# Block 0's last two output tiles as one pair by seven products, in a hybrid decoder kernel

## The reference

```python
u = rms_norm(h, g_mix[i])
z = u @ w_in[i]
...
h = h + jnp.concatenate([y_lru, y_pool], axis=-1) @ w_out[i]
v = rms_norm(h, g_ffn[i])
up = causal_dwconv(v @ w_up[i], w_conv_ffn[i], b_conv_ffn[i])
h = h + (jax.nn.gelu(gate) * val) @ w_down[i]
...
h = h + jax.nn.sigmoid(q @ w_ple_gate[i] + b_ple_gate[i]) * (p[i] @ w_ple_proj[i])
```

## Time and profile before

| | before |
|---|---|
| runs | 2138.32, 2137.21, 2137.34 us |
| median | 2137.34 us |
| the profiled execution's own time | 2137.18 us |
| its span, first to last instruction | 2135.4 us |
| granted TensorE clock, mean | 0.997 |
| TensorE busy | 2111.9 us (99%), 9274 matmuls |
| VectorE busy | 1511.0 us (71%) |
| ScalarE busy | 880.2 us (41%) |
| GpSimd busy | 380.9 us (18%) |
| HBM | 250.75 MB read, 175.11 MB written |

### The profile page before, as it was taken

The page is one execution under the profiler, slowest core; times in us unless marked ns, Lnnn a source line. Parts: engine busy times, 40 slices in busy tenths (PEclk is TensorE's granted clock), DMA queues, the critical chain, the costliest instruction groups (busy, mean ns, idle before and its releaser), DMA issues.

```text
span 2135.4 us, 24401 instructions
## 1 busy us (share of the span) xinstructions
PE 2111.9 (99%) x9274; PEld 1740.6 (82%) x9274; DVE 1511.0 (71%) x1726; ACT 880.2 (41%) x1143; POOL 380.9 (18%) x712
## 2 busy tenths in 40 slices
PE   8999999999999999999999999999999999999997
PEld 6888888888888888888888888888888888888885
DVE  7785597685858677687787796874655647574876
ACT  5764364351525344355444652532313131323343
POOL 1001102112112212211100112122222222221210
PEclk9999999999999999999999999999999999999998
DMA  6436646565656556577434356466666666666645
GB/s 239 148 143 258 225 168 228 215 257 210 236 204 264 223 213 243 202 279 270 178 123 157 99 206 198 146 191 196 192 193 197 191 194 195 190 196 193 204 158 184
DMA packets 138149, 427.49 MB, mean 200 GB/s; under 512 B 15921, under 2 KB 16049, under 8 KB 138033
## 3 DMA queue, kind: packets, MB, share of 16 engines
q0 software_dynamic: 94784, 327.20, 44.3%
q1 hardware_dynamic: 40944, 90.33, 12.9%
q10 hardware_dynamic: 2304, 8.39, 1.0%
HBM read 250.75 MB, written 175.11 MB: 199 GB/s over the span
## 4 chain that ended last, share of the span: by engine, by line
PE 97%; DVE 2%; ACT 0%; DMA 0%; issue 0%; SPq 0%; DVEq 0%; ACTq 0%
PE slot L731 45%; PE slot L914 39%; PE slot L994 11%; PE slot L788 2%; PE slot L822 1%; DVE H L2415 0%; DMA XN<-xT 0%; PE slot L845 0%; PE slot L856 0%; DVE wpair L1671 0%; DMA split_panels<-wpair 0%; ACT L1107 0%; DVE Ulo L1706 0%; DVE WV L2386 0%; DVE H L2389 0%
## 5 line engine op out<-in xcount | busy, mean ns | idle before, releaser
L914 PE MATMUL slot<-ops,wpair 128*128 128x512 f32 x3696 | 841.9, 389 | 0.4 <-ACT WG L1397 0.2
L914 PEld LDWEIGHTS slot<-ops,wpair 128*128 128x128 f32 x3696 | 693.1, 188 | 147.2 <-ACT WG L1384 2.7
L731 PE MATMUL slot<-Uhi,wpair 128*128 128x512 f32 x1176 | 318.9, 390 | 1.2 <-DVE Ulo L1706 1.2
L691 POOL DMA_DIRECT2D split_panels<-wpair x274 | 146.1, 534 | 833.1 <-DVE wpair L1671 808.0
L716 POOL DMA_DIRECT2D wpair<-split_panels x266 | 143.3, 539 | 726.2 <-PE slot L914 305.6
L731 PE MATMUL slot<-f_split,wpair 128*128 128x512 f32 x1152 | 262.1, 389 | 0.0
L731 PEld LDWEIGHTS slot<-Uhi,wpair 128*128 128x128 f32 x1176 | 220.5, 188 | 48.7 <-DVE Ulo L1706 2.0
L731 PEld LDWEIGHTS slot<-f_split,wpair 128*128 128x128 f32 x1152 | 216.2, 188 | 44.9
L994 PE MATMUL slot<-f_quarter,wpair 128*128 128x512 f32 x1008 | 229.5, 389 | 0.0
L994 PEld LDWEIGHTS slot<-f_quarter,wpair 128*128 128x128 f32 x1008 | 189.2, 188 | 39.3
L1099 ACT ACTIVATE wpair<-raw 128x512 fp32r<-128x512 f32 x186 | 113.7, 624 | 257.9 <-PE slot L731 157.8
(11 more groups left out here) (225 smaller groups left out, 2485.2 us busy)
## 6 DMA issues: line engine op xcount, KB each, us to landing
split_panels<-wpair POOLq DMA_DIRECT2D x274, 512.0 KB, 4.6
wpair<-split_panels POOLq DMA_DIRECT2D x266, 512.0 KB, 3.6
raw<-panels SPq DMA_DIRECT2D x208, 256.0 KB, 4.2
wpair<-down_sums POOLq DMA_DIRECT2D x56, 256.0 KB, 2.9
wlo_sum<-down_sums POOLq DMA_DIRECT2D x56, 256.0 KB, 3.0
down_sums<-raw POOLq DMA_DIRECT2D x42, 256.0 KB, 3.2
H<-xT SPq DMA_DIRECT2D x8, 1024.0 KB, 11.1
pp_kept<-XQ ACTq DMA_DIRECT2D x16, 512.0 KB, 3.9
```

The costliest lines, as they stand in the source:

```text
L691: pool.dma_start(split_d[n], wpair[n % RING][:].bitcast(F32)).then_inc(split_kept[n % RING], 16)
L731: mm = pe.matmul(ps[:, h * BANK:(h + 1) * BANK], stat_[:, w], mov(part, h), start=first and i == 0, stop=last and i == 2)
L914: mm = pe.matmul(ps, stat_[:, w], (lo if part else hi)[:, k, :], start=first and k == 0 and i == 0, stop=k == KP - 1 and i == 2, skip_grou ...
```

## The change

Block 0's output tiles 6 and 7 are made as one pair by seven products (`OUT_SEVEN = ((6,), (4, 6))`).

- **TensorE**: two tiles of 48 matmuls become seven products of 12. The waits of `out_by_seven` now stand in block 0 too.
- **Panels**: four raw panels stay, in the order (6,0), (7,0), (7,1), (6,1), but seven panels go through the ring: P1, P2 and P4 are raw ones, P5, P6, P3 and P7 are sums made by `wsummed`. All seven are stored split, and block 1 reads them for its own tiles 6 and 7 as it does any panel (one load of 512 KB, and no `o_sum_lo`). The separate sums of this pair (`weight_sums`, four stores) are gone. Those of tiles 4 and 5 stay, behind tile 3's addition. The plan puts P1 and P5 behind tile 4, P6 and P3 behind tile 5, P7, P2 and P4 behind P1, P5 and P6.
- **VectorE in block 0** gets the four sums of activations (ten operations of 128 by 2048) and their four low parts. The sum for P5 comes first of all, ahead of tile 0's addition. The three operations of P7's sum stand behind `ss_add` of tiles 3, 4 and 5. The first product's addition stands behind the third of them.
- **ScalarE in block 0** gets the four high parts. The layer inputs' high and low parts (`p_hi_tiles`, `p_lo_tiles`) move ahead of `refill` of tile 1.
- **Block 1**: four `o_sum_lo` of the second pair are gone, and the rest of the order stays.

The core of the diff:

```diff
-OUT_SEVEN = (4, 6)
+OUT_SEVEN = ((6,), (4, 6))
+OUT_PAIRS = [(b, m) for b in range(BLOCKS) for m in OUT_SEVEN[b]]
+OUT_SUMMED = (4,)
...
-            if not b or m < OUT_SEVEN[0]:
+            if m < OUT_SEVEN[b][0]:
                 projection(b, "out", m)
-            elif m in OUT_SEVEN:
+            elif m in OUT_SEVEN[b]:
                 job(b, "outs", m)
-                for name, _ in PRODUCTS:
-                    panel((b, "outs", m, name), None)
+                a11, a21, a22, a12 = (raw(("out", m + row, i)) for row, i in ((0, 0), (1, 0), (1, 1), (0, 1)))
+                panel((b, "outs", m, "P1"), a11)
+                panel((b, "outs", m, "P5"), None, (a21, a22))
+                panel((b, "outs", m, "P6"), None, (None, a11))
+                panel((b, "outs", m, "P3"), None, (a12, None))
+                panel((b, "outs", m, "P7"), None, (a11, a21))
+                panel((b, "outs", m, "P2"), a12)
+                panel((b, "outs", m, "P4"), a22)
...
-                            pe.wait_ge(out_added, o_count(m, behind))
+                            pe.wait_ge(out_added, o_count(b, m, behind))
                         if name in O_AT:
-                            pe.wait_ge(o_ready, O_SPLIT.index(name) + 1)
+                            pe.wait_ge(o_ready, b * len(O_AT) + O_SPLIT.index(name) + 1)
...
+            def pair_squares(b, m):
+                for name, _ in PRODUCTS:
+                    refill(b, "outs", m, name)
+                    if name == "P2":
+                        act.wait_ge(out_added, o_count(b, m, name))
+                        square(b, 1, m)
+                act.wait_ge(*out_of((b, "outs", m)))
+                square(b, 1, m + 1)
+
+            def first_out_phase(b):
+                act.wait_ge(pe_step, STEP[b, "G", GROUPS - 1, 1])
+                refill(b, "out", 0)
+                o_hi_part(b, "P5")
+                out_square(b, 0)
+                o_hi_part(b, "P6")
+                p_hi_tiles(b)
+                refill(b, "out", 1)
+                out_square(b, 1)
+                refill(b, "out", 2)
+                out_square(b, 2)
+                o_hi_part(b, "P4")
+                for m in range(3, OUT_SEVEN[b][0]):
                     refill(b, "out", m)
-                    if b:
-                        act.wait_ge(pe_step, STEP[b, "G", GROUPS - 1, 1])
-                        if m != 1:
-                            o_hi_part(O_FORMED[max(m - 1, 0)])
-                        if m == OUT_SEVEN[0] - 1:
-                            o_hi_part(O_FORMED[-1])
-                    if m == 1:
-                        p_hi_tiles(b)
-                    act.wait_ge(*out_of((b, "out", m)))
-                    square(b, 1, m)
-                for m in OUT_SEVEN if b else ():
-                    act.wait_ge(out_added, o_count(m, "P2"))
-                    square(b, 1, m)
-                    act.wait_ge(*out_of((b, "outs", m)))
-                    square(b, 1, m + 1)
+                    out_square(b, m)
+                o_hi_part(b, "P7")
+                pair_squares(b, OUT_SEVEN[b][0])
...
-                for m in range(DT):
-                    out_evicted(b, m)
-                    refill(b, "out", m)
-                    if m + 1 in OUT_SEVEN:
-                        weight_sums(out_group(m + 1), ("S1", "S3", "S2", "S4"))
-                    if m == 1:
-                        p_lo_tiles(b)
-                        dve.wait_ge(p_ready, PLE_TILES)
-                        chain.link(v.memset(WG[:, 0:HALO_FFN], 0.0))
-                        chain.link(v.memset(WV[:, 0:HALO_FFN], 0.0))
-                    ss_add(b, 1, m)
+                m6 = OUT_SEVEN[b][0]
+                o_formed(b, "P5")
+                out_evicted(b, 0)
+                refill(b, "out", 0)
+                out_evicted(b, 1)
+                o_formed(b, "P6")
+                o_lo_part(b, "P5")
+                p_lo_tiles(b)
+                refill(b, "out", 1)
+                dve.wait_ge(p_ready, PLE_TILES)
+                chain.link(v.memset(WG[:, 0:HALO_FFN], 0.0))
+                chain.link(v.memset(WV[:, 0:HALO_FFN], 0.0))
+                ss_add(b, 1, 1)
+                out_evicted(b, 2)
+                refill(b, "out", 2)
+                ss_add(b, 1, 2)
+                o_formed(b, "P4")
+                o_lo_part(b, "P6")
+                out_evicted(b, 3)
+                refill(b, "out", 3)
+                weight_sums(out_group(4), ("S1", "S3", "S2", "S4"))
+                ss_add(b, 1, 3)
+                o_formed(b, "P7", 0)
+                out_evicted(b, 4)
+                refill(b, "out", 4)
+                ss_add(b, 1, 4)
+                o_formed(b, "P7", 1)
+                out_evicted(b, 5)
+                refill(b, "out", 5)
+                ss_add(b, 1, 5)
+                o_formed(b, "P7", 2)
+                for name, _ in PRODUCTS:
+                    out_add(b, m6, name)
+                    refill(b, "outs", m6, name)
+                    if name == "P1":
+                        o_lo_part(b, "P7")
+                    if name == "P6":
+                        o_lo_part(b, "P4")
+                ss_add(b, 1, m6)
+                ss_add(b, 1, m6 + 1)
                 ss_lo_part(b, 1)
 
-            def o_formed(name):
+            def o_formed(b, name, part=None):
 
                 k_half, h = {"P5": (0, 1), "P6": (1, 1), "P4": (1, 0), "P7": (1, 1)}[name]
                 less = {"P5": (0, 0), "P7": (0, 1)}.get(name)
                 dst = o_raw[name][:]
                 if less:
-                    chain.link(v.tensor_tensor(dst, f32(y_quarter(0, k_half, h)), f32(y_quarter(0, *less)), ALU.subtract))
-                    chain.link(v.tensor_tensor(dst, dst, f32(y_quarter(1, k_half, h)), ALU.add))
-                    v.tensor_tensor(dst, dst, f32(y_quarter(1, *less)), ALU.subtract).then_inc(o_sum, 1)
+                    if part in (None, 0):
+                        chain.link(v.tensor_tensor(dst, f32(y_quarter(0, k_half, h)), f32(y_quarter(0, *less)), ALU.subtract))
+                    if part in (None, 1):
+                        chain.link(v.tensor_tensor(dst, dst, f32(y_quarter(1, k_half, h)), ALU.add))
+                    if part in (None, 2):
+                        v.tensor_tensor(dst, dst, f32(y_quarter(1, *less)), ALU.subtract).then_inc(o_sum, 1)
...
-                o_sum_lo(b, second, "P5")
                 out_add(b, first, "P4")
                 ss_add(b, 1, first)
-                o_sum_lo(b, second, "P6")
                 out_add(b, second, "P1")
-                o_sum_lo(b, second, "P3")
                 out_add(b, second, "P5")
-                o_sum_lo(b, second, "P7")
                 out_add(b, second, "P6")
```

More of the change, by code:

```diff
@@ L286 @@
 KEPT_AT, IN_COUNT, SUM_TURN = {}, {}, {}
-GROUP_RAWS = [[RAW_AT["out", m + row, i] for row in range(2) for i in range(2)] for m in OUT_SEVEN]
+GROUP_RAWS = [[RAW_AT["out", m + row, i] for row in range(2) for i in range(2)] for m in OUT_SUMMED]
 GROUP_RAWS += [[RAW_AT["down", c, i, kind] for kind in DOWN_KINDS] for c in range(BY_SEVEN) for i in range(2)]
@@ L306, in kept_panels @@
             continue
-        seven = key[1] in ("down", "outs")
+        seven = key[1] == "down" or key[1] == "outs" and key[2] in OUT_SUMMED
         name = key[3] if seven else None
@@ L313, in kept_panels @@
         else:
-            if key[1] == "outs":
+            if seven and key[1] == "outs":
                 kind = DOWN_PLAIN[name]
@@ L685, in _ @@
             sums_behind = {PANEL[0, "down", c, i, "21"]: down_group(c, i) for c in range(BY_SEVEN) for i in range(2)}
-            sums_behind.update({PANEL[0, "out", m + 1, 1]: out_group(m) for m in OUT_SEVEN})
+            sums_behind.update({PANEL[0, "out", m + 1, 1]: out_group(m) for m in OUT_SUMMED})
             pool.wait_ge(x_in[3], 16)
@@ L1049, in _ @@
                 out_opening(b)
-                for m in range(2, OUT_SEVEN[0] if b else DT):
+                for m in range(2, OUT_SEVEN[b][0]):
                     projection((b, "out", m), Yhi, Ylo)
-                for m in OUT_SEVEN if b else ():
+                for m in OUT_SEVEN[b]:
                     out_by_seven(b, m)
@@ L1308, in out_phase, with second_out_phase @@
+            def second_out_phase(b):
+                act.wait_ge(pe_step, STEP[b, "G", GROUPS - 1, 1])
+                o_hi_part(b, "P5")
+                out_square(b, 0)
+                p_hi_tiles(b)
+                out_square(b, 1)
+                o_hi_part(b, "P6")
+                out_square(b, 2)
+                o_hi_part(b, "P4")
+                o_hi_part(b, "P7")
+                out_square(b, 3)
+                for m in OUT_SEVEN[b]:
+                    pair_squares(b, m)
                 ss_hi_part(b, 1)
@@ L1637, in _ @@
                 mix(b)
-                out_phase(b)
+                if b:
+                    second_out_phase(b)
+                else:
+                    first_out_phase(b)
                 ffn(b)
```

(17 more changed lines are left out.)

39 lines of the change are left out of this document (20 added, 19 removed).

## The result

The changed kernel takes 2143.64 us (median; 2142.23 to 2146.12), the kernel before 2137.38 us in the same comparison (2136.96 to 2139.38). The ratio is 1.0029, with a 95% interval from 1.0020 to 1.0038: 6.3 us slower. The forecast was 2144.1, 0.5 above the measured median and within its range. The nine executions of the changed kernel lie within 3.9 us, the nine of the kernel before within 2.4.

A forecast was written before the change was run, and what follows sets the result against it. TensorE was taken to bound the kernel, busy 2111.9 of 2135.4 us. 2137.18 - 2.72 - 0.34 + 0.25 + 6.9 + 2.7 = 2143.97, as a median of runs 2144.1 us; range 2139.5 to 2147.5.

The forecast's parts named there:

- Matmuls, tiles 2 and 4: TensorE in block 0: 12 matmuls fewer, 2.72 us less; tile 2 0.25 us later; tile 4's late start gone, 0.34 less.
- P6 behind P1's addition: Block 0's pair: TensorE's product P6 waits for VectorE to add P1, starting at 238.7 instead of 231.8, 6.9 us more.
- the load's term: VectorE ahead of P5's weight sum: it waits 2.3 us for raw panels, between 0 and 3.3.
- 34.0 us of work: VectorE's operations from 197.84 up to P1's addition, which would put that addition at 231.9 without a single wait.
- without the load's wait it is 4.6: Block 0's pair: P6 would be 4.6 us late if VectorE did not wait for raw panels ahead of P5's sum.
- The prediction's 3.3: P6's lateness in us without the raw panels' wait and with the panel of 197.17 also coming before 196.5.
- its second rival: Block 0's pair: shorter waits, P6 waiting 1 to 4 us and P3 up to 2.7; 2137 to 2141.5 us, chance 17%.
- P3 behind P5's addition: Block 0's pair: P3 waits for P5's addition, queued on VectorE behind P7's sum, panel and low part; 2.7 us more.
- The third rival: Block 0's pair: TensorE's clock falls in the wait, P6 takes 5.4 us, P3 2.7 more; 2146.8 us, chance 13%.
- Behind the pair and block 1: After block 0's pair no wait at `stat`, nothing, up to 0.5 us; block 1's saved low parts worth nothing.
- VectorE keeps up: Rival: TensorE waits nowhere in block 0's pair, P1's addition starting by 230.9; 2134.3 us, chance 8%.

The follow-up runs named there:

- The new order: Changed kernel with VectorE's and ScalarE's operations in block 0's output projection reordered by two lists, none added or dropped; 2134.21 us, ratio 0.9984 to the kernel before.
- less work: Changed kernel without two of VectorE's 2048-column operations in block 0 (in P7's and P4's sums), 4.5 us of work; 2142.78 us, ratio 1.0022.
- the load's wait filled: Changed kernel with P7's second sum operation and P1's low part moved ahead of P5's weight sum on VectorE; 2142.33 us, ratio 1.0021.
- P1's addition first: Changed kernel with only P1's addition moved ahead of tile 5's sum of squares and P7's last sum operation; 2145.18 us, ratio 1.0037.
- TensorE kept busy: Changed kernel with 24 matmuls without use added behind P5, in block 0 only; 2145.18 us, ratio 1.0032.
- both additions first: Changed kernel with P1's and P5's additions moved ahead of tile 5's sum of squares and P7's last sum operation; 2143.67 us, ratio 1.0033.

## Why the prediction was right

**Matmuls, tiles 2 and 4: right.** 12 matmuls fewer. Tile 2 comes 0.19 late (predicted 0.25: its four matmuls take 1.26 instead of 1.07), and tile 4's 1.41 of the earlier trace rows is 1.07 now. The new order gives this part by itself: block 1's pairs start at 1274.57 there against 1278.07 in the earlier trace rows, with an opening 0.40 earlier (34.35 against 34.75), so 3.10 are won. 2.72 + 0.34 is 3.06.

**P6 behind P1's addition: right in size.** Predicted 6.9 late, measured 6.06. P1's addition was put at 237.7 and stands at 237.37, of which 0.45 is this execution's late opening. Its parts, predicted and measured from start to start: loads behind pair 4's sums later by 4.1, and 4.17 (218.98 against the 214.81 of the earlier trace rows, 0.45 of it the opening); standing for the raw panels 2.3, and 1.62 (222.29 - 220.07 less the 0.60 of P1's low part); a panel's way over ScalarE 0.88 more, and 0.86 to 0.88, three times; two squares 0.35 each, and 0.35 and 0.34. So the load's term was 0.7 too large, and the others came out. The step from the addition to P6 was 0.16 too large: 0.94, and 0.78 measured. The two make up the 0.8. The whole sum is 6.8 us (2143.97 - 2137.18) against 6.0 in the accounting; that the forecast lies within 0.5 of the median is partly the difference between single executions.

**Its reason: only in part right.** The prediction summed 34.0 us of work and the waits since 197.84, as if any of these microseconds would bring P1's addition forward (it has 3.3 where 1.3 more go), and it took the load's wait for 2.3 of the 6.9. The experiments show the step that fails: tile 5's addition can't start before tile 5's matmuls end, and from there to P1's addition there are 9.2 us of program against 5.4 us of TensorE's. With less work the sum is: 0.20 from the start of the pair (226.72) to tile 5's addition, 9.20 to P1's, 0.78 to P6, less 5.44 for P1 and P5, 4.74. It is also 4.74 with the load's wait filled (236.19 - 226.01 - 5.44), and by this reason it stays whatever comes before. All the rest, work and load together, is 6.06 - 4.74 = 1.3. So the sentence "without the load's wait it is 4.6" is right in its number by luck: the floor lies there. The prediction's 3.3 lies below the floor, and so do the 1 to 4 us of its second rival; with this order behind tile 5's addition neither could come.

**P3 behind P5's addition: right, and not a price of its own.** Predicted 2.7, measured 2.72. The prediction says that it shrinks only where P6's wait nearly vanishes. With P1's addition first, P6's wait fell to 2.24 and P3's rose to 6.37. The two are one lateness, set by P5's addition and, where that one comes first too, by P6's, which stands behind P7's low parts (3.22 ahead of P7).

**The clock: it fell, and cost nothing that shows.** The third rival had it fall and add 2.7 at P3. It fell (windows of the changed kernel, columns as above; P6 starts at 238.15, P3 at 243.59):

```profile
232.00:238.00 6.00, 0.25 (x2) 0.00 (x0) 4.97 (x6) 2.09 (x3) 0.94 (x2) 0.83 0.43 175
238.00:241.00 3.00, 2.85 (x7) 2.30 (x8) 1.70 (x4) 2.44 (x3) 0.00 (x0) 0.50 0.00 0
241.00:244.00 3.00, 2.71 (x9) 1.88 (x8) 3.00 (x4) 0.63 (x1) 0.53 (x1) 0.70 0.64 196
244.00:247.00 3.00, 3.00 (x15) 2.47 (x14) 3.00 (x4) 0.39 (x1) 1.07 (x2) 1.00 0.90 324
```

P6 took 5.14, which P3's wait took in: 0.29 of the predicted 2.7 us is left in the view of waits. P3 took 246.41 - 243.59 = 2.82 instead of 2.72, at a granted clock of 1.00. That 0.1 is not the clock's: P6 took 3.00 instead of 2.88 behind 0.32 us of idling with TensorE kept busy, at 1.00 too. The prediction had the cover right, and the rival's second half did not come: the clock is back before P3. The Trainium skill (TensorE: Matmul & The Clock Gate, What's actually happening) has the throttled clock as the default and activity as what releases it; the windows above agree, and the sum did not change by it, because the matmuls that ran slowly stood ahead of another wait. Where none follows it does cost: 1.77 with P1's addition first, 1.68 with TensorE kept busy, 1.73 behind P7 with both additions first, each with about that 0.1 in it. (There P6's 1.69 was taken in by P7's wait.)

**Behind the pair and block 1: right.** `ss_part` was put at 262.3 and is done at 260.80 + 1.22 = 262.02; `stat`'s four matmuls follow `pp`'s without a gap at 262.73. Block 1's pairs take 38.08 in both kernels, so its four saved low parts are worth nothing there.

**VectorE keeps up: not in this order.** The first rival needed P1's addition by 230.9, where work alone gave 231.9. Its 2134.3 is what the new order measures (2134.21, with 3.65 us won against its own kernel before where the rival has 3.06), with P1's addition at 228.58. The same work fits; it stood in the wrong places.

Open: why P6 runs at full clock after a wait of 2.24 us in one kernel and slowly after 2.02 in another, and which of the moves of the new order were needed.

## What to carry to other kernels

To price a late release, find the last event that the releasing engine can't get ahead of, and count what its program has between that and the release; work taken away before that event wins only until the engine idles there (4.5 us less work won 1.3). Two waits behind one engine's queue are one lateness: moving one operation forward passes it on to the next product (a wait of 6.4 us), moving two passes it on to the one after (7.3 us late there instead of 8.9). It went when the whole stretch was laid out anew, with more of what doesn't depend on the late event ahead of it and other work in each handover (9.4 us, with the same operations); whether fewer moves would do is not shown. In these traces a slow clock behind a wait was paid only where no second wait covered it, so look at what follows before filling the wait.

## What the hardware showed that was not expected

The clock fell in long waits and behind short ones. Ahead of P3 in the kernel with TensorE kept busy, TensorE was idle for 0.32 and then 2.44 us with P6's 12 matmuls between, and P3 took 4.40 us from its start to P7's. With both additions first, 12 matmuls took 4.57 us behind 2.02 us of idling, and the granted clock was still 1.00 over the idle time (232.9 to 234.9) and 0.52 from 235.5 to 239.0: it fell when the matmuls were already running again. It did so again behind the 3.22 us ahead of P7 (1.00 from 242.2 to 245.4, 0.50 from 246 to 249). But with P1's addition first, 12 matmuls took 3.00 behind 2.24 us. A product's row at full clock is 2.88. P6's row took 5.14 and 4.35 in two executions of the changed kernel, 5.46 with less work and 4.58 with the load's wait filled, behind waits of 5.91, 6.29, 4.58 and 4.58. So the length of the wait does not tell how much is lost, between 0.1 and 2.6 us for 12 matmuls.
